# A transformer-style block on one core: the feed-forward in two parts, with smaller activation buffers

## What is computed

```python
D_MODEL, D_FF, SEQ = 2048, 5632, 256

def _swiglu(h, w_gu, w_down):
    gate, up = jnp.split(h @ w_gu, 2, axis=-1)
    return (jax.nn.silu(gate) * up) @ w_down

x = x + 0.5 * _swiglu(_rmsnorm(x, ffn1_norm[l]), ffn1_w_gu[l], ffn1_w_down[l])
x = x + _token_mixing(...)
x = x + 0.5 * _swiglu(_rmsnorm(x, ffn2_norm[l]), ffn2_w_gu[l], ffn2_w_down[l])
# second block, for each of two layers, with c_act = silu(c):
mod = c_act @ w_ada[l] + b_ada[l]
```

## Time and profile before

| | us |
|---|---|
| time, median of 3 runs | 3026.06 (3023.61 to 3027.93) |
| profiled execution, first to last instruction | 3022.0 |
| TensorE busy | 3001.6 (99%) |
| DVE busy | 1983.5 (66%) |
| ACT busy | 1449.2 (48%) |
| POOL busy | 1326.5 (44%) |
| granted clock, mean | 0.998 |

### The profile page before, as it was taken

How to read it: one execution, slowest core, us unless ns; L and a number is a source line. 1 busy time by engine, 2 the same in 40 slices (tenths; PEclk the granted TensorE clock), 3 DMA queues, 4 the chain that set the end, 5 groups by cost and what they waited for, 6 DMA issues and landing times.

```text
span 3022.0 us, 46302 instructions
## 1 busy us (share of the span) xinstructions
PE 3001.6 (99%) x18688; PEld 2660.7 (88%) x18688; DVE 1983.5 (66%) x2918; ACT 1449.2 (48%) x1885; POOL 1326.5 (44%) x653
## 2 busy tenths in 40 slices
PE   9999999999999999999999999999999999999998
PEld 7888888888999999998888888888899998999997
DVE  4777665664324457777566666577579866789764
ACT  6444444444657455544544444444544454544454
POOL 5455545445565555585554555444550004710013
PEclk9999999999999999999999999999999999999999
DMA  7888887886776555566688888788576546665555
GB/s 241 274 279 264 273 282 252 290 287 182 226 175 175 158 165 150 151 170 199 214 274 285 268 272 268 263 291 279 172 216 195 161 143 213 183 192 182 154 181 181
DMA packets 491662, 663.33 MB, mean 220 GB/s; under 512 B 70440, under 2 KB 278040, under 8 KB 490936
## 3 DMA queue, kind: packets, MB, share of 16 engines
q1 hardware_dynamic: 485960, 655.85, 68.5%
q0 software_dynamic: 4448, 2.94, 0.3%
q10 hardware_dynamic: 1040, 1.58, 0.2%
HBM read 656.06 MB, written 2.11 MB: 218 GB/s over the span
## 4 chain that ended last, share of the span: by engine, by line
PE 96%; DVE 3%; ACT 0%; issue 0%; POOL 0%; DMA 0%; DVEq 0%; ACTq 0%
PE ps L1088 37%; PE ps L952 20%; PE ps L1093 18%; PE ps L958 10%; PE ps L969 3%; PE ps L974 1%; PE ps L936 1%; DVE narrow_split_slabs L2132 1%; PE ps L1571 1%; PE ps L1350 1%; PE ps L1331 1%; DVE h_split L2089 1%; PE ps L1059 0%; DVE U L2082 0%; PE ps L1358 0%; PE ps L1388 0%
## 5 line engine op out<-in xcount | busy, mean ns | idle before, releaser
L880 POOL TENSOR_TENSOR split_slabs<-stage,split_slabs 128x1024 fp32r<-128x1024 f32 x318 | 775.4, 2439 | 1289.3 <-ACT split_slabs L1627 1289.2
L1627 ACT ACTIVATE split_slabs<-stage 128x1024 fp32r<-128x1024 f32 x592 | 627.3, 1061 | 858.7 <-PE ps L1093 790.8
L1088 PE MATMUL ps<-split_slabs,h_split 128*128 128x512 f32 x3288 | 813.1, 389 | 0.0
L1627 ACT ACTIVATE narrow_split_slabs<-stage 128x1024 fp32r<-128x1024 f32 (+1 forms) x437 | 457.7, 1051 | 611.0 <-PE ps L958 460.6
L1088 PEld LDWEIGHTS ps<-split_slabs,h_split 128*128 128x128 f32 x3288 | 616.9, 188 | 127.9
L2132 DVE TENSOR_TENSOR split_slabs<-stage,split_slabs 128x1024 fp32r<-128x1024 f32 x274 | 354.0, 1292 | 493.0 <-ACT split_slabs L1627 491.1
L952 PE MATMUL ps<-h_split,narrow_split_slabs 128*128 128x256 f32 x4928 | 620.6, 279 | 2.9 <-issue 1.9
L952 PEld LDWEIGHTS ps<-h_split,narrow_split_slabs 128*128 128x128 f32 x4928 | 586.0, 188 | 14.5 <-issue 8.7
L880 POOL TENSOR_TENSOR narrow_split_slabs<-stage,narrow_split_slabs 128x1024 fp32r<-128x1024 f32 (+1 forms) x182 | 441.2, 2434 | 317.5 <-ACT narrow_split_slabs L1627 317.1
L1093 PE MATMUL ps<-split_slabs,h_split 128*128 128x512 f32 x1644 | 439.4, 389 | 0.0
L2132 DVE TENSOR_TENSOR narrow_split_slabs<-stage,narrow_split_slabs 128x1024 fp32r<-128x1024 f32 x255 | 339.5, 1335 | 126.8 <-ACT narrow_split_slabs L1627 125.7
(11 more groups left out here) (309 smaller groups left out, 2516.9 us busy)
## 6 DMA issues: line engine op xcount, KB each, us to landing
stage<-in_ffn_w_gu SPq DMA_DIRECT2D x352, 512.0 KB, 4.9
stage<-in_w_in SPq DMA_DIRECT2D x349, 512.0 KB, 3.9
U<-in_w_ada SPq DMA_DIRECT2D x192, 512.0 KB, 5.4
stage<-in_ffn_w_down SPq DMA_DIRECT2D x176, 512.0 KB, 5.1
stage<-in_w_out SPq DMA_DIRECT2D x96, 512.0 KB, 4.2
stage<-in_w_in SPq DMA_DIRECT2D x80, 128.0 KB, 2.8
stage<-in_w_branch_c SPq DMA_DIRECT2D x32, 192.0 KB, 3.5
stage<-in_cmp_w SPq DMA_DIRECT2D x8, 512.0 KB, 4.9
```

What stands on the lines that cost most here:

```text
L880: nc.gpsimd.tensor_tensor(slab_part(n, 1, size(n)), stage[:, n % RING, 0:size(n)], slab_part(n, 0, size(n)).bitcast(F32), ALU.subtract).th ...
L1088: mm(ps[:, 2 * pair + T, :], stationary(kk, i)[:, T * P:(T + 1) * P], w[0][:, kk, :], start=first and kk == 0 and i == 0, stop=False)
L1627: return fn(slab_part(n, 0, size(n)), stage[:, n % RING, 0:size(n)], ACT.Copy)
```

## The change

The feed-forward is done in two parts. Gate and up groups 0 to 5 come first, then the down product over their 24 chunks: 4 column groups of 12 slabs. Then groups 6 to 10, and the down product over their 20 chunks: 4 column groups of 10 slabs. Each down product adds half its sums to x, so x is updated twice. `act_split` is cut from 44 to 24 chunks for each of its two halves. The number of slabs and their contents stay, their order in the stream changes. x is squared, turned and rounded only in the last part. In the down products the steps at slab 10 and 11 move to 8 and 9. The 32 late ada loads are spread over both down products, from slab 10 of each on.

```diff
+PARTS = ((0, 6), (6, 11))
+ACT_CHUNKS = 4 * max(j1 - j0 for j0, j1 in PARTS)
-FFN_SLABS, FFN_GROUPS = GU_SLABS + DOWN * DOWN_GROUPS, GU_GROUPS + DOWN_GROUPS
+FFN_SLABS, FFN_GROUPS = GU_SLABS + DOWN * DOWN_GROUPS, GU_GROUPS + len(PARTS) * DOWN_GROUPS
+PART_DOWN = [2 * (j1 - j0) for j0, j1 in PARTS]
+def gu_at(j):
+    return 16 * j + DOWN_GROUPS * sum(PART_DOWN[:part_of(j)])
+def down_at(p):
+    return 16 * PARTS[p][1] + DOWN_GROUPS * sum(PART_DOWN[:p])
...
 def ada_places():
-    free = [i for i in range(25, GU_SLABS) if i % 16 not in range(3, 9)]
+    free = [gu_at(j) + q for j in range(1, GU_GROUPS) for q in range(16) if q not in range(3, 9) and (j, q) >= (1, 9)]
     early = [free[m * len(free) // ADA_EARLY] for m in range(ADA_EARLY)]
+    free = [down_at(p) + i for p in range(len(PARTS)) for i in range(10, DOWN_GROUPS * PART_DOWN[p] - (8 if p else 0))]
     late = ADA_LOADS - ADA_EARLY
-    return early + [GU_SLABS + 9 + m * (DOWN * DOWN_GROUPS - 24) // late for m in range(late)]
+    return sorted(early + [free[m * len(free) // late] for m in range(late)])
...
-LGT = 8192
+LGT = AT - SHIFT + 2 * ACTS
-        ats = over("act_split", [P, 2, FC * S], F32R, u_at + AT - SHIFT)
+        ats = over("act_split", [P, 2, ACTS], F32R, u_at + AT - SHIFT)
...
-        by_vector -= {s + 16 * j + 5 for s in (S_F1, S_F2) for j in range(1, GU_GROUPS + 1)}
+        by_vector -= {s + gu_at(j) + 5 for s in (S_F1, S_F2) for j in range(1, GU_GROUPS) if j != PARTS[1][0]}
+        by_vector -= {s + down_at(p) + 5 for s in (S_F1, S_F2) for p in range(len(PARTS))}
...
 # TensorE
+                def down(part):
+                    s1, g1, per, last_j = s0 + down_at(part), g0 + down_group(part), PART_DOWN[part], GU_GROUPS * f + PARTS[part][1]
+                    for d in range(DOWN_GROUPS):
+                        if d == 0:
+                            pe.wait_ge(silu_done, last_j)
+                            pe.wait_ge(act_lo, last_j - 1)
                         else:
+                            pe.wait_ge(evacuated, g1 + d - 1)
+                        for q in range(per):
+                            n = s1 + per * d + q
+                            if d == 0 and q == per - 2:
+                                pe.wait_ge(act_lo, last_j)
...
+                for part, (j0, j1) in enumerate(PARTS):
+                    for j in range(j0, j1):
+                        gate_and_up(j)
+                    down(part)
 # ACT
+                def down(part):
+                    per, last = PART_DOWN[part], part == len(PARTS) - 1
+                    for i in range(per * DOWN_GROUPS):
+                        round_upto(s0 + down_at(part) + i)
+                        if i == 8:
+                            round_act(f, PARTS[part][1] - 1)
+                        if last and i >= per and i % per == 6:
+                            squares(r + 1, i // per - 1)
+                        if last and i >= per and i % per == 8:
+                            if f == 0:
+                                round_h(1, i // per - 1, pcol("mix_norm", 0, DC))
+                            else:
+                                round_raw(0, i // per - 1)
 # DVE
+                        if (j, q) == (PARTS[1][0], 3):
+                            residual(0, DOWN_GROUPS - 1)
...
+                def down(part):
+                    j, per, last = PARTS[part][1] - 1, PART_DOWN[part], part == len(PARTS) - 1
+                    for i in range(per * DOWN_GROUPS):
+                        if i == 3:
+                            gated(j)
+                        between(down_at(part) + i)
+                        if 4 <= i < 8:
+                            turn_act(j, i - 4)
+                        if i == 9:
+                            rest_act(j)
+                        if i >= per and i % per == 3:
+                            residual(part, i // per - 1)
+                        if last and f == 1 and i == per + 3:
+                            shift_columns(0, ((0, DC - 1), (DC - 1, DC)))
+                        if last and i >= per and 4 <= i % per < 8:
+                            turn_block(r + 1, i // per - 1, i % per - 4)
+                        if last and i >= per and i % per == 9:
+                            if f == 0:
+                                rest_h(1, i // per - 1, pcol("mix_norm", 0, DC))
+                            else:
+                                rest_raw(0, i // per - 1)
```

More of the change, by code:

```diff
@@ L71, in bank_pairs @@
     pairs = []
-    for first, groups, ups in ((G_F1, FFN_GROUPS, GU_GROUPS), (G_MIX, MIX_GROUPS, 0), (G_F2, FFN_GROUPS, GU_GROUPS),
-                               (G_LAY[0], LAY_GROUPS, 0), (G_LAY[1], LAY_GROUPS, 0)):
+    ffn = [ups for j0, j1 in PARTS for ups in (j1 - j0, -DOWN_GROUPS)]
+    for first, runs in ((G_F1, ffn), (G_MIX, [-MIX_GROUPS]), (G_F2, ffn), (G_LAY[0], [-LAY_GROUPS]), (G_LAY[1], [-LAY_GROUPS])):
         start = 1 - pairs[-1] if pairs else 0
-        pairs += [1 - start] * ups + [(start + i) % 2 for i in range(groups - ups)]
+        for n in runs:
+            pairs += [1 - start] * n if n > 0 else [(start + i) % 2 for i in range(-n)]
     return pairs
@@ L213 @@
 SILU = AT + 2 * FC * S
+ACTS = ACT_CHUNKS * S
 ADA_RING = SILU + 2 * WN
@@ L491, in ffn_slabs @@
         def ffn_slabs(w_gu, w_down):
[L492 to L496, removed]
+            for j0, j1 in PARTS:
+                for j in range(j0, j1):
+                    wide_slabs(w_gu, j * WN)
+                    wide_slabs(w_gu, FF + j * WN)
+                for g in range(DOWN_GROUPS):
+                    wide_slabs(w_down, g * WN, 2 * j0, 2 * j1)
         def stream():
@@ L1713, in ffn_act, with gate_and_up @@
             def ffn_act(f, s0, g0, r):
-                for j in range(GU_GROUPS):
+                def gate_and_up(j):
                     for q in range(16):
-                        round_upto(s0 + 16 * j + q)
-                        if j > 0 and q == 10:
+                        round_upto(s0 + gu_at(j) + q)
+                        if j not in (PARTS[0][0], PARTS[1][0]) and q == 10:
                             round_act(f, j - 1)
@@ L2234, in ffn_vec @@
                             log_sigmoid(j - 2)
[L2235 to L2251, removed]
-                        else:
-                            rest_raw(0, i // DOWN - 1)
+                def down(part):
[17 more added lines that the diff above has]
+                                rest_h(1, i // per - 1, pcol("mix_norm", 0, DC))
+                            else:
+                                rest_raw(0, i // per - 1)
@@ L2254, in ffn_vec @@
+                for part, (j0, j1) in enumerate(PARTS):
+                    for j in range(j0, j1):
+                        gate_and_up(j)
+                    down(part)
                 modulation(f)
-                residual(DOWN_GROUPS - 1)
+                residual(len(PARTS) - 1, DOWN_GROUPS - 1)
             def modulation(f):
```

73 lines of the change are left out of this document (36 added, 37 removed).

## The result

The changed kernel takes 3043.82 us (median of 4 runs, 3041.47 to 3051.38) against 3025.11 for the kernel before on the same chip: a ratio of 1.0065, interval 1.005 to 1.0079. It is slower by 18.7 us; the forecast was 9.4 us slower. Both are single executions, and executions of one kernel differ by a few us.

What follows compares the result with a forecast made beforehand. TensorE, multiplying weight slabs without a gap, was taken to bound the kernel. Profiled 3022.0 us plus waits of 3.5 and 6.0 us gave 3031.5, so 3035.5 us as a median; range 3025.5 to 3046 us.

Steps and rivals of the forecast that it cites:

- the beat and the cushion: Down products: TensorE takes a slab every 2.72 us; DVE's remainder is ready 7.4 us before TensorE asks for it.
- What was costed at nothing: Eight more residuals, up groups overwriting activations, ada loads in gate and up groups, POOL's slabs: covered, 0 us.
- The hand-over at 8/9: Last activation rounded at slab 8, remainder at 9: 1.6 us to spare in part 1, so 0 us.
- DVE in part 1: Last down product: DVE's work in 10-slab groups plus POOL collisions makes TensorE wait 3.5 and 6.0 us per feed-forward.
- Rival C: Gaps let TensorE's clock fall, two slabs after each of three gaps at half speed: +16 on top, 3051 us; chance 0.03.
- A clock below 1.00: Listed among the signs that would show the forecast wrong; gaps of 1 to 2 us in 27 were expected to keep 1.00.
- the second block's remainders at 1.7 us and one meeting with POOL: Last down product: a block's four remainders priced at 1.7 us, with up to 2.4 us for a meeting with POOL.
- dearer block remainders (+17): Upper bound: block remainders costing 2.6 us of their own instead of 1.7 give waits of 7 and 10 us, +17.
- a hand-over that slips (+3): Upper bound: DVE reaches the last residual late and delays the next stage, 3 us more, making +20.
- Rival A: The cushion holds: DVE's backlog never passes 7.4 us and TensorE never waits; 3026.1 us, not slower; chance 0.25.
- Rival B: Hand-over to the next stage slips: last residual and norm delayed, 1 to 2 us more per feed-forward, 3038.5 us; chance 0.05.

Runs made afterwards that it cites:

- each cure: Two runs on the changed kernel: late ada loads moved to quiet slabs of the last part, 3027.69 us; x blocks turned into PSUM instead of SBUF, 3027.93 us.
- The version with both cures: The changed kernel with late ada loads moved away from the dense slabs and x blocks turned into PSUM: 3027.39 us, ratio 1.0005.
- The version with both cures and a late hand-over: Changed kernel with ada loads moved, x blocks in PSUM, and the last part's activation steps at slabs 10 and 11 instead of 8 and 9: 3040.63 us.
- The experiment with PSUM: The changed kernel, ada places unchanged, with DVE turning the x blocks into two PSUM banks instead of SBUF: 3027.93 us, ratio 1.0011.
- the first experiment: The changed kernel with the 32 late ada loads re-placed, 24 in the first down product and 8 at quiet slabs of the last: 3027.69 us, ratio 1.0007.
- the groups of 12 slabs: The changed kernel with the parts reversed, groups 0 to 4 first, then 5 to 10, so the last down product has 12-slab groups: 3031.89 us, ratio 1.0022.

## Why the prediction was right in kind and short in size

- **TensorE bounds, and the beat and the cushion.** Confirmed. TensorE's new gaps all lie in the last parts, slab 21 of the first feed-forward was 7.4 us late and cost TensorE 0.1 to 0.2, and each cure that kept the lateness under that brought nearly all the time back.
- **What was costed at nothing** (eight residuals, gated groups, POOL's slabs, ada places in the other groups). The version with both cures has all of it and shows no gap; by its times it costs 4 us at most.
- **The hand-over at 8/9.** 1.6 us to spare was predicted. In the changed kernel the last down product starts at 623.77, DVE's activation remainder ends at 642.59 + 1.28 = 643.87 and TensorE takes slab 8 at 645.53: 1.7 us to spare. Made two slabs late, it opened a gap of 5.1 us a time.
- **DVE in part 1.** The place and the releasers were right: slabs 27, 29 and 31 in the first feed-forward, 21 and 31 in the second; nothing in part 0. The gaps came to 5.7 + 5.9 = 11.6 us instead of 3.5 + 6.0 = 9.5. Slabs 19, 25, 27 and 29 of the second, listed with 0.2 to 1.0 us each, opened none; slabs 21 and 31 took more, so that its sum came out by two errors that cancel. DVE wasn't always busy either: it waited some 1.15 us for ACT at 672.99 and at 704.60.
- **The step that failed most: matmuls behind a gap at full speed, which the sum put at nothing (Rival C, 0.03).** Of the 10.1 us that the sum lacks (19.6 - 9.5), the gaps' length is 2.1 and TensorE's longer busy time 8.2. Some 5.9 of these are the passes right behind three gaps, at granted clocks of 0.51 to 0.64 over 4 us. A clock below 1.00 was one of the prediction's own signs of being wrong, and the last parts show 0.99 and 0.96. It priced Rival C at +16, from two whole slabs at half speed behind each gap; measured was somewhat over a third of that. It took two stretches, one nearly full and one half idle, and concluded that a full one with short gaps would keep its clock. The version with both cures and a late hand-over shows this cost by itself, 2.0 to 2.3 us behind a gap of 5.1. The Trainium skill (TensorE: Matmul & The Clock Gate, "HAM oscillation — how this bites in real kernels") warns of such a fall between bursts; the granted clocks of 0.50 to 0.64 in the rows above bear it out.
- **The smaller error: the second block's remainders at 1.7 us and one meeting with POOL.** They took 5.98 us, two meetings, and the gap at slab 31 grew from 2.2 to 4.4 and 3.7 us. The row had shown a single instruction at 2631 ns against 477. It wasn't asked whether POOL's next subtraction would begin before the four were through. It did (behind the first block 0.37 us after the one before it, at 676.85), and DVE was shut out again. The experiment with PSUM, where the same instructions never exceed 483 ns in the first feed-forward, shows the collision to be a cause.
- **The range held the result for another reason than it gives.** Its upper end is made of dearer block remainders (+17) and a hand-over that slips (+3). The hand-over didn't slip, and the gaps were 11.6 us and not 17; what filled the rest was the clock, which the range left out. That 3043.82 lies under 3046 is partly luck.
- **The two terms together.** 11.6 us of gaps and 5.9 of slow passes are 17.5 of the 19.6. About half of the rest is TensorE getting under way behind each gap: slab 27's 0.74 us set it back by 1.04 (slab 28 began at 701.15, and 697.39 + 2.72 is 700.11). An estimate from such rows is some 1 us for the five gaps. What remains wasn't taken apart.
- **Rival A** (the lateness never passes the cushion) is not what the changed kernel does; it is what either cure brings about. **Rival B** isn't in the changed kernel's profile, but was in that of the first experiment.

## What to carry to other kernels

When a helper's work is packed into shorter groups, carry its lateness forward slab by slab against the cushion, and count a collision for every operation of the neighbour that can begin before the group is through: here two for four short instructions. Then move the work that has no due time out of the dense places, before touching the tiling: here one change of the place table brought back some 16 of 18.7 us, in part because an engine that is on time again meets its neighbour less often. And give each long gap (2.2 us and more here) a second term, for the slow matmuls behind it: in the changed kernel it was nearly a third of the loss.

## What the runs showed of the hardware

- Four DVE instructions of 0.48 us, both inputs in SBUF, took 5.97 us beside two POOL subtractions of 2.5 us, 3.8 with one such subtraction and 2.38 beside the end of one. With one input in PSUM none exceeded 483 ns in the first feed-forward, though POOL was subtracting during the first two blocks. The Trainium skill has the exclusion (SBUF — State Buffer, "SBUF: two separate sides": a lock held for the whole instruction); that a group of short instructions is shut out more than once is what these rows add.
- The clock behind a gap doesn't follow from the gap's length alone. The gaps of 3.73, 4.37 and twice 5.11 us were each followed by eight passes of 2.52 to 3.78 us instead of 1.98, and that of 2.26 us in the first experiment by 16 matmuls in 3.58 instead of 2.16; after those up to 1.88 us the passes ran at full rate again at once (1.99 us after the one of 1.88). At 2.17 us it went both ways: in the changed kernel at 2121.92 the next eight passes took 3.11 us, while with the groups of 12 slabs TensorE went on at full rate, at a granted clock of 1.00:

```profile
2132.97 1.19 PE L1128 MATMUL ps<-split_slabs,act_split 128*128 128x512 f32 x4 [2.17 <-DVE split_slabs L2182]
2134.00 1.99 PE L1123 MATMUL ps<-split_slabs,act_split 128*128 128x512 f32 x8
```
```profile
2134.00:2138.00 4.00, 4.00 (x19) 3.32 (x18) 3.93 (x5) 0.00 (x0) 1.17 (x1) 1.00 0.86 291
```

  What decides at that length stays open; no run was made for it.
